# A split-product output projection, modulation sums moved into value products, and bias loads from another queue, in a four-layer transformer kernel

## The chip, the cores and the metric

One NeuronCore of one Trainium2 chip runs the whole program in one launch. The metric is the device time in microseconds (us). A profiled execution gives the trace; its times are read from one run.

## The reference

Four layers work on a sequence of 256 tokens of width 1024, in fp32. Each layer is a mixer and a mixture of experts, both added to the rows x. Layers 1 and 2 have 32 experts, layers 3 and 4 have 16. Layers 3 and 4 are modulated: `mod = silu(c) @ w_ada + b_ada` gives, for each of the two layers, six vectors of 1024 (shift, scale and gate of the mixer, shift, scale and gate of the experts), so `w_ada` is 1024 x 12288.

The change touches layer 3 above all, the dilated attention:

```
hm = rmsnorm(x, norm_mix) * (1 + sc_m) + sh_m
proj = (hm @ w_in).reshape(b, s, 3 groups, 3 of q/k/v, 16 heads, 64)
# for each group (window, dilation): logits = q.k + bias[bucket(distance)], masked, softmax
# the three groups of a head are merged by their softmax denominators
o = sum_g weight_g * out_g
x = x + g_m * (o @ w_out)
```

## The kernel before

**Stream.** All weights pass through one SBUF ring of 28672 fp32 columns per partition (14 slots of 1 MB). `Stream.add` lays the chunks out in the order of use, and gives each the number of chunks that must have been given back before it may be loaded (`need`). SyncE issues the loads (L96, `stream.issue`), waits on the counter `chunk_used`, and its last argument bounds for how many returned chunks it may wait at this point. An expert is three pieces of 1 MB. A chunk of `w_ada` is 3 MB, and there are 16 of them (`ada_at`); `weight_amid` places them between chunks of a weight. Layer 2's `w_out` has two 3 MB chunks, layer 3's `w_in` 18 chunks of 2 MB (nine for each half of the heads) and its `w_out` two of 2 MB.

**Modulation.** `ada_part` (L434 to L441) does the six sums of one `w_ada` chunk on VectorE, each a multiply with a row of silu(c) and a sum over 1024 columns (L438). The row is loaded by `load_silu_row` (L431). `modulation` turns the sums into `mod` and the gains. Before, chunks are summed in the output projections of layer 1 (3), 2 (2), 3 (3) and 4 (3), and five in input stages.

**Output projection.** `project_rows` (L452 on) does, for two 512-wide column blocks and two row blocks of 128 tokens, k fp32 matmuls of 128x128 by 128x512 each (L508; k is 12 in layer 2 and 8 in layer 3; the program runs each as two instructions). VectorE multiplies by the gate and adds to x (L1333, L1334), between its `ada_part` calls; ScalarE takes squares for the next norm (L543). With a gate, 8 small matmuls first spread it over rows (L500).

**Layer 3.** Two halves of eight heads, each of them `project_heads_split` and then `dilated_attention`. The first has nine jobs of 512 columns: q and k of three groups (six jobs, normed, scaled and transposed), then the value products of the three groups. Each weight row block is split in two fp32r halves: `high` is a copy by ScalarE (L859), `low` the difference by VectorE (L911). The same is done to the source (GpSimd makes its low part, L791). TensorE then does three products high*high, high*low and low*high (L826), six instructions for each of eight row blocks. There are three buffers for split weights, so `high` of block n waits for the products of block n-3.

`dilated_attention` (L1145 on) works on pairs of heads, i = 0 to 3. TensorE makes scores (L1187), transposes probabilities (L1220) and multiplies by the values (L1230). VectorE adds the bias and takes the extreme (L1260), scales (L1268) and copies the result out (L1287). ScalarE takes the exponentials (L1299) and copies the transposes out of PSUM (L1307, function `take`). Its order in one pass of the loop is two `take`s of pair i-1, `exp(i, 0)`, four `take`s of pair i-1, `exp(i, 1)`. The bias of a pair is six DMAs of 128 KB (L3091). The first two pairs are loaded during the value products; those of pairs 2 and 3 are issued by SyncE inside the attention, when the logits of pair i-2 are done:

```
@block.sync
def _(sp):
    for i in range(2, n):
        sp.wait_ge(*logits_ready[1].at(2 * (i - 1)))
        for y in range(2):
            bias_load(2 * i + y, bias[i][y], bias_loaded[i % 2].sem)
```

Every `nc.Block` ends with all engines meeting. After the projection comes `moe(2, ...)`, with 16 experts in eight pairs.

## Time and profile before

| what | value |
|---|---|
| median of 3 runs | 1508.71 us (1507.35 to 1511.42) |
| profiled execution, its own time | 1510.9 us |
| its span | 1509.2 us |
| mean granted TensorE clock | 0.984 |
| TensorE busy | 1410.7 us, 93% |
| VectorE, ScalarE, GpSimd busy | 736.5, 496.6, 103.0 us |
| DMA | 469.80 MB, mean 311 GB/s |

The stages by the trace: layer 2's output projection from 523 to 565 us, its experts until about 790; layer 3's first half with products from 801.5 to 907.6 and attention from 908.6 to 949.15; its second half with products from 951.0 to 1056.6 and attention from 1057.6 to 1098.67; its output projection from 1098.67 to 1130.16; its experts until 1241; then layer 4. A busy TensorE means that a matmul was in flight, not that the array was full; idle time of an engine that nobody waits for costs nothing.

### The profile page before, as it was taken

To read this page: it belongs to the slowest core of one execution; us is meant where nothing else is said; L and a number is where in the kernel's file an instruction comes from. 1 tells how busy PE (TensorE), PEld (TensorE's weight loads), DVE (VectorE), ACT (ScalarE), POOL (GpSimd) and SP (SyncE) were. 2 spreads that over 40 slices of the span, in tenths; PEclk is the share of its full clock that TensorE was granted. 3 is DMA by queue.
4 is the path that set the end of the run, shared out by engine and by line. 5 is a ranking of instruction groups with operands and counts; after the bars stand their busy time and mean duration, and the time that the engine had idled before them with its cause. 6 is when DMAs were issued, how large, how long until landed. Compare 5 with 4: busy or idle time off the path is not lost. (4 is left out here: it accounts for less than half of the span.)

```text
span 1509.2 us, 23584 instructions
## 1 busy us (share of the span) xinstructions
PE 1410.7 (93%) x9090; PEld 766.4 (51%) x9090; DVE 736.5 (49%) x1659; ACT 496.6 (33%) x996; POOL 103.0 (7%) x258
## 2 busy tenths in 40 slices
PE   8999999997899899999888997899799998989998
PEld 4486533332365645333226885788554337755432
DVE  1468332222255545222226765675576346669534
ACT  3222221111216403111116656665613126661211
POOL 0000021110000001111102000200001102000110
PEclk9999999999999999999999999999999999999999
DMA  8996989999974269999998463335369998437996
GB/s 365 366 348 265 405 360 411 420 420 421 427 301 167 97 290 370 398 422 420 421 423 347 168 251 112 112 140 192 116 243 419 420 425 324 162 119 296 422 420 247
DMA packets 63400, 469.80 MB, mean 311 GB/s; under 512 B 7809, under 2 KB 15921, under 8 KB 18738
## 3 DMA queue, kind: packets, MB, share of 16 engines
q1 hardware_dynamic: 63282, 468.22, 76.7%
q8 instruction: 75, 1.23, 0.3%
q14 instruction: 43, 0.35, 0.1%
HBM read 465.42 MB, written 2.76 MB: 310 GB/s over the span
## 5 line engine op out<-in xcount | busy, mean ns | idle before, releaser
L1663 PE MATMUL PS<-ring,catT 128*32 128x512 f32 x3072 | 347.9, 594 | 11.8 <-issue 10.9
L826 PE MATMUL PS<-w_split,h_split 128*128 128x512 f32 x1152 | 270.9, 394 | 6.0 <-DVE w_split L911 5.9
L826 PEld LDWEIGHTS PS<-w_split,h_split 128*128 128x128 f32 x1152 | 214.1, 188 | 56.5 <-DVE w_split L911 8.6
L1663 PEld LDWEIGHTS PS<-ring,catT 128*32 128x32 f32 x3072 | 96.0, 110 | 227.5 <-issue 227.2
L911 DVE TENSOR_TENSOR w_split<-ring,w_split 128x512 fp32r<-128x512 f32 x192 | 132.7, 706 | 67.3 <-ACT w_split L859 67.1
L1686 PE MATMUL PS<-ring,row_place 128*32 128x512 f32 x1232 | 141.8, 593 | 14.1 <-issue 14.1
L859 ACT CAST w_split<-ring 128x512 fp32r<-128x512 f32 x192 | 118.3, 621 | 104.5 <-PE PS L826 104.1
L1873 ACT ACTIVATE row_place<-PS 128x256 f32<-128x256 f32 x48 | 18.5, 385 | 359.7 <-PE PS L1663 359.7
L508 PE MATMUL PS<-ring,catT 128*128 128x512 f32 x224 | 96.7, 592 | 1.0 <-PEq L1022 1.0
L1686 PEld LDWEIGHTS PS<-ring,row_place 128*32 128x32 f32 x1232 | 40.9, 110 | 105.0 <-issue 104.4
L1556 POOL COPY catT<-xsT 128x256 f32 x176 | 63.3, 403 | 393.0 <-PE PS L1663 385.4
L2058 DVE TENSOR_TENSOR row_place<-PS,row_place 128x256 f32<-128x256 f32 x48 | 20.3, 422 | 130.8 <-ACT row_place L1873 130.8
L2062 DVE COPY row_place<-PS 128x256 f32<-128x256 f32 x48 | 20.4, 424 | 111.6 <-PE PS L1672 111.6
L508 PEld LDWEIGHTS PS<-ring,catT 128*128 128x128 f32 x224 | 42.3, 190 | 53.3 <-issue 53.3
L438 DVE CUSTOM_DVE_ANT_0 ring<-ring,row_place 128x1024 f32<-128x1024 f32 x48 | 55.6, 1223 | 5.9 <-DMA row_place<-silu_dram 5.5
L2083 DVE SCALAR_TENSOR_TENSOR gated_rows<-PS,slot_w,grow 128x512 f32<-128x512 f32 x32 | 24.0, 750 | 67.3 <-PE PS L1686 67.3
L2090 DVE SCALAR_TENSOR_TENSOR xn_split<-PS,slot_w,xn_split 128x512 fp32r<-128x512 f32 x36 | 27.0, 751 | 48.9 <-ACT xn_split L1860 48.9
L1537 POOL MEMSET xsT<- 128x512 f32 x4 | 2.1, 526 | 637.2 <-POOLq L476 507.7
L2605 PE MATMUL PS<-ring,catT 128*128 128x512 f32 x96 | 41.7, 594 | 1.3 <-DVE catT L2497 0.9
L438 DVE CUSTOM_DVE_ANT_0 ring<-ring,silu_row 128x1024 f32<-128x1024 f32 x36 | 41.7, 1222 | 1.3 <-PE PS L2404 1.3
L1860 ACT ACTIVATE xn_split<-PS,slot_w 128x512 fp32r<-128x512 f32 x36 | 24.8, 689 | 51.8 <-PE PS L1686 51.8
L791 POOL TENSOR_TENSOR h_split<-hT,h_split 128x256 fp32r<-128x256 f32 x24 | 24.3, 1023 | 232.9 <-ACT h_split L869 230.3
(445 smaller groups left out, 1829.4 us busy)
## 6 DMA issues: line engine op xcount, KB each, us to landing
ring<-in_moe SPq DMA_DIRECT2D x269, 1024.0 KB, 14.3
ring<-in_w_ada SPq DMA_DIRECT2D x16, 3072.0 KB, 13.0
ring<-in_a_w_in SPq DMA_DIRECT2D x23, 2048.0 KB, 10.4
ring<-in_b_w_in SPq DMA_DIRECT2D x8, 2048.0 KB, 22.5
first_down<-in_moe SPq DMA_DIRECT2D x8, 1024.0 KB, 8.4
ring<-in_a_w_out SPq DMA_DIRECT2D x2, 3072.0 KB, 15.2
ring<-in_b_w_out SPq DMA_DIRECT2D x2, 3072.0 KB, 16.5
ring<-in_w_mem_kv SPq DMA_DIRECT2D x2, 2048.0 KB, 11.6
```

The source lines that it names most:

```text
L438: last = nc.vector.tensor_tensor_reduce(w[:, m, :], w[:, m, :], row, 1.0, 0.0, ALU.mult, ALU.add, ada_out[:, 6 * c + m:6 * c + m + 1])
L508: last = nc.tensor.matmul(PS[:, i % 8, 0:n], srcT[:, j, t * P:(t + 1) * P], w[:, j, o:o + n], start=j == 0, stop=j == k - 1)
L791: nc.gpsimd.tensor_tensor(hs[:, 1, k, :], srcT[:, k, :], hs[:, 0, k, :].bitcast(F32), ALU.subtract).then_inc(h_low.sem, 1)
L826: last = nc.tensor.matmul(PS[:, 2 * (i % 2) + t, :], hs[:, hp, k, t * P:(t + 1) * P], wk[:, (KT * i + k) % splits, wp, :], start=k == 0 an ...
L859: nc.scalar.copy(wk[:, (KT * i + k) % splits, 0, :], w[:, k, :]).then_inc(w_high.sem, 1)
L911: nc.vector.tensor_tensor(wk[:, (KT * i + k) % splits, 1, :], w[:, k, :], wk[:, (KT * i + k) % splits, 0, :].bitcast(F32), ALU.subtract).t ...
L1556: nc.gpsimd.tensor_copy(xf[:, i % 2, :, q * HALF:(q + 1) * HALF], padded(q // 2)[:, :, bass.ds(at, HALF)]).then_inc(win_ready.sem, 1)
L1663: last = nc.tensor.matmul(PS[lanes, 4 + i % 2, :].rearrange("p (g f) -> p g f", g=2), xf[:, i % 2, k, lanes], gate_up_weights(2 * i + q % ...
L1686: last = nc.tensor.matmul(PS[lanes, 6 + c, :], hs[:, i % 2, f2, lanes], down_weights(2 * i + q % 2, f2)[:, c * BANK:(c + 1) * BANK], start ...
L1860: nc.scalar.activation(yk(i, 0, c), PS[:, 6 + c, :], ACT.Copy, scale=slot_w[:, i % 2, :]).then_inc(y_high.sem, 1)
L2090: nc.vector.scalar_tensor_tensor(yk(i, 1, c), PS[:, 6 + c, :], slot_w[:, i % 2, :], high, ALU.mult, ALU.subtract).then_inc(y_low.sem, 1)
L2605: last = nc.tensor.matmul(PS[:, bank, :], catT[:, k, t * P:(t + 1) * P], w[:, k, :], start=n == 0, stop=n == 11)
```

## The change

There are four edits.

1. Layer 3's output projection is done by a new function, `project_rows_split`, with the three fp32r products and four buffers for split weights. It has no modulation sums and doesn't load the silu row. The last three row blocks of the second column block are done for one row block of tokens and then for the other.
2. The three `w_ada` chunks that layer 3's output projection summed are gone from there. One is summed in each half, in the value products: one of its six sums behind the `low` of each of six weight blocks (jobs 7 and 8). ScalarE's queue issues the load of the silu row for it, behind the root of the last normed job, into the place of the squares.
3. The third goes to layer 2's output projection, which then sums three chunks in place of two: one ahead of the first column block, two ahead of the second.
4. The bias DMAs of pairs 2 and 3 are issued by ScalarE, behind `exp(i, 1)` of pairs 0 and 1; SyncE's loop is gone.

The order of chunks in the ring changes with 2 and 3.

```diff
-        c_bout = weight_amid("b_w_out", 12, [512] * 2, [1, 0], 1)
+        c_bout = weight_amid("b_w_out", 12, [512] * 2, [1, 1], 1)
-        c_ain2 = weight("a_w_in_2", 8, [512] * 18)
-        c_aout2 = weight_amid("a_w_out_2", 8, [512] * 2, [1, 0], 2)
+        c_ain2 = weight_amid("a_w_in_2", 8, [512] * 18, [0] * 8 + [1] + [0] * 8 + [1])
+        c_aout2 = weight("a_w_out_2", 8, [512] * 2)
...
+        def ada_sum(c, m, row):
+            w = stream.view(ada_at[c], 6)
+            return nc.vector.tensor_tensor_reduce(w[:, m, :], w[:, m, :], row, 1.0, 0.0, ALU.mult, ALU.add, ada_out[:, 6 * c + m:6 * c + m + 1])
...
+        def project_rows_split(srcT, k, first, gate, router, after, gain=None, shift=None, splits=4):
...
+                HELD = 3
+                @block.sync
+                def _(sp):
+                    wr, br = router_weights(router)
+                    nc.sync.dma_start(wr, A[f"wr{router}"]).then_inc(r_loaded.sem, 16)
+                    nc.sync.dma_start(br, A[f"br{router}"].partition_broadcast(P)).then_inc(r_loaded.sem, 16)
+                    stream.issue(nc, sp, first)
+                    load_early_down(router, (0, 1))
...
+                    stream.issue(nc, sp, first + 1)
+                @block.gpsimd
+                def _(pool):
+                    for j in range(k):
+                        pool.wait_ge(*(h_odd if j % 2 else h_even).at(j // 2 + 1))
+                        nc.gpsimd.tensor_tensor(hs[:, 1, j, :], srcT[:, j, :], hs[:, 0, j, :].bitcast(F32), ALU.subtract).then_inc(h_low.sem, 1)
+                @block.tensor
+                def _(pe):
+                    def product(c, j, t, h, w):
+                        return nc.tensor.matmul(PS[:, 2 * c + t, :], hs[:, h, j, t * P:(t + 1) * P], wk[:, (k * c + j) % splits, w, :],
+                                                start=j == 0 and h == 0 and w == 0, stop=j == k - 1 and h == 1)
...
+                    for c in range(2):
+                        held = k - HELD if c else k
+                        for j in range(held):
+                            if c == 0:
+                                pe.wait_ge(*(h_odd if j % 2 else h_even).at(j // 2 + 1))
+                            pe.wait_ge(*w_high.at(k * c + j + 1))
+                            for t in range(TT):
+                                product(c, j, t, 0, 0)
+                            pe.wait_ge(*w_low.at(k * c + j + 1))
+                            for t in range(TT):
+                                product(c, j, t, 0, 1)
+                            if c == 0:
+                                pe.wait_ge(*h_low.at(j + 1))
+                            for t in range(TT):
+                                last = product(c, j, t, 1, 0)
...
+                            last.then_inc(w_used.sem, 1)
+                        for t in range(TT if held < k else 0):
+                            for j in range(held, k):
...
+                                for h, w in ((0, 0), (0, 1), (1, 0)):
+                                    last = product(c, j, t, h, w)
+                            last.then_inc(rows_ready.sem, 1)
...
+                @block.scalar
+                def _(act):
...
+                    nc.scalar.activation(stat[:, 2, 30:31], ones_f[:, 0:1], ACT.Sqrt)
+                    for j in range(0, k, 2):
+                        nc.scalar.copy(hs[:, 0, j, :], srcT[:, j, :]).then_inc(h_even.sem, 1)
+                        high(0, j)
+                        high(0, j + 1)
+                    for j in range(k):
+                        high(1, j)
+                    for i in range(3):
+                        square(i)
...
+                    for j in range(0, k, 2):
+                        nc.vector.tensor_copy(hs[:, 0, j + 1, :], srcT[:, j + 1, :]).then_inc(h_odd.sem, 1)
+                        low(0, j)
+                        low(0, j + 1)
+                        if j == 4:
...
+                                nc.vector.tensor_copy(gain, PS[:, 6:8, :].rearrange("p b n -> p (b n)")).then_inc(gate_made.sem, 1)
...
+                            after()
+                    for j in range(k):
+                        low(1, j)
+                        if j == splits - 1:
+                            add(0)
+                        if j == splits:
+                            add(1)
+                    add(2)
+                    add(3)
...
 # project_heads_split, ScalarE and VectorE
+                            if sums_behind and i == turns[-1]:
+                                nc.scalar.dma_start(silu_row, A["silu_dram"].to_broadcast([P, D])).then_inc(silu_loaded.sem, 16)
...
+                            if (i, k) in sums_behind:
+                                m = sums_behind.index((i, k))
+                                if m == 0:
+                                    dve.wait_ge(*silu_loaded.at(16))
+                                    dve.wait_ge(*stream.landed(ada_at[ada_chunk]))
+                                last = ada_sum(ada_chunk, m, silu_row)
+                                if m == 5:
+                                    dlink(last)
+                                    nc.vector.sem_inc(chunk_used, 1)
...
 # dilated_attention
-                @block.sync
-                def _(sp):
-                    for i in range(2, n):
-                        sp.wait_ge(*logits_ready[1].at(2 * (i - 1)))
-                        for y in range(2):
-                            bias_load(2 * i + y, bias[i][y], bias_loaded[i % 2].sem)
...
                         if i < n:
                             exp(i, 1)
+                        if i + 2 < n:
+                            act.wait_ge(*logits_ready[1].at(2 * (i + 1)))
+                            for y in range(2):
+                                bias_load(nc.scalar, 2 * (i + 2) + y, bias[i + 2][y], bias_loaded[i % 2].sem)
...
-            project_rows(catT, 12, c_bout, [512] * 2, add_rows(None), ada=[1, 0], ada_last=1, ...)
+            project_rows(catT, 12, c_bout, [512] * 2, add_rows(None), ada=[1, 1], ada_last=1, ...)
...
+                        project_heads_split(hT, c_ain2 + half * 10, jobs, ..., ada_chunk=11 + half, sums_behind=((7, 3), (7, 5), (7, 7), (8, 1), (8, 3), (8, 5)), ...)
...
-            project_rows(catT, 8, c_aout2, [512] * 2, add_rows(grow[:]), ada=[1, 0], ada_last=2, after=..., router=2, gate=mod[:, 0, 16:24], shift=mod[:, 0, 24:32])
+            project_rows_split(catT, 8, c_aout2, mod[:, 0, 16:24], 2, lambda: modulation(1, (0, 24), (0,)), grow[:], mod[:, 0, 24:32])
```

## Rows read from the trace of the kernel before

**Rows 1.** Page, part 1: busy time of each engine, share, instructions.

```profile
PE 1410.7 (93%) x9090; PEld 766.4 (51%) x9090; DVE 736.5 (49%) x1659; ACT 496.6 (33%) x996; POOL 103.0 (7%) x258
```

**Rows 2.** Busy by window: stretch, length, PE, PEld, DVE, ACT, POOL, clock, DMA.

```profile
1098.67:1130.16 31.49, 31.18 (x96) 15.81 (x96) 27.79 (x47) 3.67 (x8) 0.00 (x0) 1.00 0.76 286
908.60:949.15 40.55, 31.81 (x312) 23.66 (x312) 21.82 (x60) 24.40 (x58) 0.00 (x0) 0.92 0.21 76
1130.16:1241.00 110.84, 109.84 (x963) 43.44 (x965) 52.57 (x143) 24.23 (x44) 12.94 (x38) 1.00 1.00 416
```

**Rows 3.** Timeline of layer 3's output projection: start, length, engine, line.

```profile
1098.68 1.28 ACT L528 ACT_TABLE_LOAD   x1 [2.99 <-PEq L1153]
1100.58 27.63 PE L508 MATMUL PS<-ring,catT 128*128 128x512 f32 x64
1128.36 0.70 DVE L1333 TENSOR_TENSOR PS<-PS,grow 128x512 f32<-128x512 f32 x1 [0.25 <-PE PS L508]
```

**Rows 4.** Groups by line, value products of the second half, 1034 to 1058.

```profile
L826 PE MATMUL PS<-w_split,h_split 128*128 128x512 f32 x96 | 22.0, 390 | 0.0
L911 DVE TENSOR_TENSOR w_split<-ring,w_split 128x512 fp32r<-128x512 f32 x14 | 9.7, 693 | 9.6 <-ACT w_split L859 9.6
L859 ACT CAST w_split<-ring 128x512 fp32r<-128x512 f32 x14 | 8.7, 624 | 8.9 <-PE PS L826 8.9
```

**Rows 5.** Timeline, start of the second half's products.

```profile
949.15 0.41 ACT L869 CAST h_split<-hT 128x256 fp32r<-128x256 f32 x1 [3.00 <-PEq L1153]
951.05 11.17 PE L826 MATMUL PS<-w_split,h_split 128*128 128x512 f32 x48 [2.67 <-DVE w_split L911]
```

**Rows 6.** Timeline: two neighbouring modulation sums.

```profile
1103.69 1.22 DVE L438 CUSTOM_DVE_ANT_0 ring<-ring,row_place 128x1024 f32<-128x1024 f32 x1
1104.83 1.22 DVE L438 CUSTOM_DVE_ANT_0 ring<-ring,row_place 128x1024 f32<-128x1024 f32 x1
```

**Rows 7.** Bias DMA issues (L3091) on SyncE: ns min/median/max.

```profile
L3091 SPq DMA_DIRECT2D z_rows<-bias_dram x24: 567/570/1462, 885.8 to 1066.8; - x24
```

**Rows 8.** Timeline of the first half's attention, behind `exp(0, 1)`.

```profile
914.40 4.56 SPq L3091 DMA_DIRECT2D z_rows<-bias_dram  x6
915.38 0.84 ACT L1307 COPY catT<-PS 128x384 f32<-128x384 f32 x2
916.91 1.54 PE L1220 MATMUL PS<-ident,logits 128*128 128x128 f32 x6 [1.78 <-DVE logits L1268]
917.85 0.48 ACT L1307 COPY probsT<-PS 128x384 f32<-128x384 f32 x1 [0.43 <-PE PS L1220]
```

**Rows 9.** The same, behind `exp(1, 1)`; the last is from the second half.

```profile
924.11 1.78 SPq L3091 DMA_DIRECT2D grow<-bias_dram  x3
925.00 0.19 ACT L1299 ACTIVATION_READ_ACCUMULATOR logits<-logits,rowmax 128x1 f32 x1
925.70 0.86 ACT L1307 COPY catT<-PS 128x384 f32<-128x384 f32 x2 [0.51 <-PE PS L1220]
927.71 0.88 PE L1220 MATMUL PS<-ident,logits 128*128 128x128 f32 x6 [1.08 <-DVE logits L1268]
928.29 0.86 ACT L1307 COPY probsT<-PS 128x384 f32<-128x384 f32 x2 [0.53 <-PE PS L1220]
1075.24 0.86 ACT L1307 COPY catT<-PS 128x384 f32<-128x384 f32 x2 [1.00 <-PE PS L1220]
```

**Rows 10.** Timeline of layer 2's output projection: VectorE's last adds.

```profile
554.22 0.69 DVE L1334 TENSOR_TENSOR x<-x,PS 128x512 f32<-128x512 f32 x1 [2.10 <-PE PS L508]
564.63 0.69 DVE L1334 TENSOR_TENSOR x<-x,PS 128x512 f32<-128x512 f32 x1 [9.72 <-PE PS L508]
```

**Rows 11.** Windows of layer 2's projection and of its experts' end.

```profile
550.00:560.00 10.00, 10.00 (x24) 4.37 (x23) 2.74 (x8) 0.73 (x2) 0.00 (x0) 1.00 0.45 186
560.00:570.00 10.00, 9.28 (x49) 6.07 (x47) 4.74 (x9) 3.59 (x6) 0.53 (x1) 1.00 0.35 121
740.00:760.00 20.00, 16.39 (x142) 5.49 (x142) 4.08 (x9) 2.30 (x4) 1.43 (x4) 1.00 1.01 422
```

More of the change, by code:

```diff
@@ L741, in project_heads, with project_heads_split @@
                 s.passed(k)
-        def project_heads_split(srcT, first, jobs, splits=3, rows=None, norm=None, side=None, load_last=None):
+        def project_heads_split(srcT, first, jobs, splits=3, rows=None, norm=None, side=None, load_last=None, ada_chunk=None, sums_behind=()):
             turns = [i for i, job in enumerate(jobs) if job["hd"]]
@@ L767, in turned_x @@
                     return PS[:, 4 + 2 * (k % 2) + k // 4, at:at + T]
+                silu_row = catT[:, 8:12, :].rearrange("p k n -> p (k n)")
                 def chunk(i):
-                    return first + i + (1 if side is not None and i >= 3 else 0)
+                    return first + i + (1 if side is not None and i >= 3 else 0) + (1 if sums_behind and i >= len(jobs) - 1 else 0)
                 def col16(q):
@@ L958, in project_heads_split @@
                 s.passed(k)
+            silu_loaded.passed(16 if sums_behind else 0)
             for s in (w_high, w_low, w_used):
@@ L3060, in build @@
                 attention([mla_head(h) for h in range(8)], True, row_scale=qs[:, 2])
-            project_rows(catT, 12, c_bout, [512] * 2, add_rows(None), ada=[1, 0], ada_last=1, after=lambda: modulation(0, (0, 48), (0, 1)), router=1)
+            project_rows(catT, 12, c_bout, [512] * 2, add_rows(None), ada=[1, 1], ada_last=1, after=lambda: modulation(0, (0, 48), (0, 1)), router=1)
         if stop >= 4:
@@ L3085, in build, with bias_load @@
                         bias = [(first_bias[:, 0], first_bias[:, 1]), (other_bias, catT[:, 5:8, :])]
-                        def bias_load(h, dst, loaded):
+                        def bias_load(eng, h, dst, loaded):
                             bd = A["bias_dram"]
@@ L3095, in load_two_biases @@
                                 for y in range(2):
-                                    bias_load(2 * i + y, bias[i][y], sig(f"bias_loaded{i}").sem)
-                        project_heads_split(hT, c_ain2 + half * 9, jobs, rows=z_rows, load_last=load_two_biases,
+                                    bias_load(nc.sync, 2 * i + y, bias[i][y], sig(f"bias_loaded{i}").sem)
+                        project_heads_split(hT, c_ain2 + half * 10, jobs, rows=z_rows, load_last=load_two_biases, ada_chunk=11 + half, sums_behind=((7, 3), (7, 5), (7, 7), (8, 1), (8, 3), (8, 5)),
                                             norm=(mod_gain[:, 0, 0, :], mod[:, 0, 0:8]) if half == 0 else None)
@@ L3106, in build @@
                         dilated_attention([head(h) for h in range(8)], bias, bias_load)
-            project_rows(catT, 8, c_aout2, [512] * 2, add_rows(grow[:]), ada=[1, 0], ada_last=2, after=lambda: modulation(1, (0, 24), (0,)), router=2, gate=mod[:, 0, 16:24], shift=mod[:, 0, 24:32])
+            project_rows_split(catT, 8, c_aout2, mod[:, 0, 16:24], 2, lambda: modulation(1, (0, 24), (0,)), grow[:], mod[:, 0, 24:32])
         if stop >= 7:
```

62 lines of the change are left out of this document (61 added, 1 removed).

## The prediction

> **What bounds the kernel now.** I read the page's first part, then the busy time by windows, then the timeline of the stages that the diff touches. TensorE is busy 1410.7 of 1509.2 us [rows 1], but that is no single limit. In layer 3's output projection it never stops (31.18 of 31.49 us) [rows 2], and the timeline shows one unbroken run of 27.63 us of fp32 matmuls, with VectorE's last gate product starting 0.25 us behind it [rows 3]: TensorE sets that stage, and VectorE's 27.79 busy us there, mostly modulation sums, lie under it. Layer 3's experts are set by TensorE too (109.84 of 110.84), although DMA is full (share 1.00) [rows 2]. The experts of layer 2 are different: from 740 to 760 TensorE has 16.39 of 20 us at 422 GB/s [rows 11]; there DMA decides. The attention is set by a ring of short steps through four engines: TensorE has 31.81 of 40.55 us at clock 0.92 [rows 2], and each step waits for another engine [rows 8, 9].
>
> **Output projection: -4.4 us.** It removes the 27.63 us run [rows 3]. In its place are 2 column blocks x 8 row blocks x 6 = 96 products. The value products ran 96 of the same in 22.0 us with no idle [rows 4], so that is the new run, 5.6 us less. It begins later. The old run began 1.91 us behind the stage's start at 1098.67. The new one needs, on ScalarE in turn, the table load (1.28, and 0.20 for the operation that calls it), a source copy 0.41 [rows 3, 5] and a weight copy 0.62, then VectorE's difference of 0.69 [rows 4]: first products at 2.6, and the low part at 3.3, when the first two products (0.46) are done and wait 0.3. That is as if the run began 2.9 behind the stage's start, 1.0 later; with 0.2 for the first block, where the second half's 48 products took 11.17 in place of 11.0 [rows 5], the net is -5.6 + 1.0 + 0.2 = -4.4. The feeders keep up: of 1.38 us that TensorE takes for a block, ScalarE needs 0.62 and half a source copy (0.2), VectorE 0.69 and half of one, and four buffers leave about three blocks of lead; the gate copy and the first adds (about 1.4 us each) fit into it. GpSimd's low parts are needed in the first block alone. The tail (router matmuls, last gate product and add) stays. Bounds: -5.6 with no start loss, -2.5 if VectorE's inserted adds are felt.
>
> **Sums in the value products: +0.5 us.** Two sums start 1.14 us apart [rows 6], so with the reading out of the sum I take 1.15 to 1.23. VectorE is busy 0.69 of each 1.38 us block [rows 4]. A sum behind every second block asks 2 x 0.69 + 1.2 = 2.6 of 2.75 us. The worst place is job 7, block 5, where a sum is followed by the last copy out of a transposed bank (0.7): the next low part is 0.69 + 1.2 + 0.7 - 1.38 = 1.2 us late. TensorE bears about 1.4: with three buffers a high part starts when the block three before is done, 0.62 + 0.69 + hops give 1.35, and TensorE comes to it after two blocks, 2.75. So nearly nothing shows; I take 0.25 per half. If nothing were hidden it would be 12 x 1.2 = 14 us, and I keep 4 of that as the upper end. The silu row's load is one issue on ScalarE, which idles 8.9 of 24 us there [rows 4].
>
> **The third chunk in layer 2: 0.** VectorE gets six more sums, 6.9 us, ahead of its add at 554.22, which would push that at most to 561.1, still ahead of the last one at 564.63, which waits 9.72 us for TensorE [rows 10]. The 3 MB go into the ring ahead of experts' pieces, before a stage that DMA decides; 3 MB at 420 GB/s are 7.5 us. But of the 20 us from 550 to 570, DMA is idle 0.55 and 0.65 of the time [rows 11], 12 us, since the ring is full. Going through `need` for both orders, 14 pieces of the experts are in the ring when the projection ends, in both kernels, and the next piece waits for the same event. The delayed 4 MB (the chunk and its place) fit into the idle 12 us. Its price if the cover failed is the 7.5 us.
>
> **Ring in layer 3: 0.** Three chunks fewer ahead of layer 3's experts let 10 pieces be loaded during the half's products, against none before the projection now. It buys nothing: TensorE waits for no DMA there [rows 2].
>
> **Bias loads on ScalarE: +6.5 us.** No row shows a DMA issued by ScalarE. The nearest rows are SyncE's for the same transfers: 0.57 us each at the median, 1.46 at most [rows 7]. Six make 3.4 us. Behind them on ScalarE stands `take(i, 0)`, for which TensorE's third transpose of the pair waits, since the PSUM bank must be free, and through it the ring of steps. The wait that the change adds is met already when `exp(i, 1)` starts (ScalarE waited for the same count), so I take it that the issue starts there, beside the exponential. For i = 0: from 914.40 to 917.8; `take` ran at 915.38, and the later `take` had 0.43 us of wait to give [rows 8], so 2.0 by ScalarE's order, 1.7 with what TensorE at its lower clock would need anyway. For i = 1: from 924.11 to 927.5; `take` ran at 925.70 with 0.53 to give later [rows 9], 1.3; in the second half `take` was 0.5 later in relation (idle 1.00 against 0.51 [rows 9]), 0.8. Sum over both halves: 1.7 + 1.7 + 1.3 + 0.8 = 5.5. Before, six transposes took 1.54 us at 916.91, after a pause of 1.78 us [rows 8], and 0.88 at 927.71 [rows 9]: TensorE was at the lower of its two levels in the first place (clock 0.92 over the stage [rows 2]). Longer pauses may lengthen that; I add 1.0. Lower bound: 1.1 us if an issue takes 0.33, as the plain loads of SyncE do, and 0 below that; nothing can be gained, since no VectorE instruction waited for a bias. Upper bound: 13 us, with SyncE's 4.56 us for six [rows 8], begun only when the exponential has ended. I take the same cost as on SyncE because the transfers are the same.
>
> The Trainium skill has two rules that pull apart here. "DMA: Bandwidth & Descriptors", section "Issuing engines are not separate DMA queues", says that spreading issues over engines only saves the sequencer's issue time, usually small beside the transfer; by it the edit costs little, and the sum would be about -3.9. "Perfetto Trace Analysis", section "Per-engine timelines", says that an issuing sequencer is held until the descriptors are generated; by it ScalarE is held as long as SyncE, which is the sum taken here. The rows of SyncE (0.57 us each) agree with the second so far as they go.
>
> **Sum.** -4.4 + 0.5 + 0 + 0 + 6.5 = +2.6 us on the profiled execution, whose own time is 1510.9. That run lies 2.2 us above the median of 1508.71; the difference is taken over unchanged: 1511.3.
>
> **Rivals.**
> - *Issue is cheap on ScalarE (0.25).* An issue of up to about 0.34 us would end before the `take` behind it plus its slack (2.1 us at i = 1), and the attention keeps its time. Then only -4.4 + 0.5 = -3.9 remain: 1504.8. For it: the descriptor work may differ. Against it: the same transfers took 0.57.
> - *The issues are felt in full (0.25), the slower side.* Place: the four issue groups in the attention. If the six issues start only when the exponential is done (925.19, 1.0 us later than the wait), each adds 1.0: +4, together +6.6, 1515.3; with more time at the lower clock 1518. It decides from the point where the last issue ends 4.2 us after its wait is met: then the four delays exceed the 3.9 us gained by 4.5.
> - *VectorE doesn't keep up in the value products (0.08).* Each sum that is felt costs up to 1.2; with 4 us, 1515. For it: 2.6 of 2.75 us asked. Against it: six sums only, and 9.6 us of idle [rows 4].
> - That the new projection doesn't gain: only if the split parts come late; the rows of the same feeders in the same order show no idle of TensorE [rows 4].
>
> **How the numbers follow.** A difference of 0.3%, 4.5 us, is about what can be told from no change. The forecast case (0.42) has its own range from 1507 to 1514. Of it 0.02 is faster, 0.33 within the bound, 0.07 slower. The cheap issue gives 0.12 faster, 0.13 same, since -3.9 lies close to the bound. Full cost: 0.23 slower, 0.02 same. VectorE: half and half. Sum: faster 0.14, same 0.52, slower 0.34. For 8 in 10 I reach from 1503.5 to 1517.
>
> **What would show it.** In the trace after: products of 22 to 22.6 us in the projection, begun 2.6 us behind its start, and the stage about 27 in place of 31.5 us; ScalarE's DMA issues of about 0.57 us each, and an idle or a lag of `take` behind `exp(i, 1)`; attentions of 43 to 44.5 us in place of 40.55 and 41.1; product stages of the halves unchanged within 0.5 us; layer 2's experts and layer 3's experts of unchanged length. The prediction is wrong if issues on ScalarE are much shorter or don't hold back the next `take`, if TensorE's low clock lasts far longer in the attention, or if layer 2's experts end later.

## The result, and the profile after

The changed kernel takes 1521.7 us (median of 11 runs, 1512.64 to 1526.39), the kernel before in the same comparison 1510.74 (11 runs, 1502.79 to 1514.76): ratio 1.007, 95% interval 1.0053 to 1.0088. The prediction said 1511.3 us, in a range from 1503.5 to 1517.0; the change is slower by 11 us, not by 2.6. The profiled execution of the changed kernel took 1517.79 us, 3.9 under its median; its span is 1515.8, 6.6 us above the span before, so it shows somewhat over half of the loss by medians.

First the page's line of busy times and the new queue, for the changed kernel; they answer to [rows 1]. The columns of the last line are packets, MB and share of 16 engines.

```profile
PE 1412.5 (93%) x9117; PEld 777.7 (51%) x9122; DVE 750.0 (49%) x1679; ACT 506.3 (33%) x1016; POOL 111.8 (7%) x266
q10 hardware_dynamic: 3552, 4.20, 0.9%
```

TensorE is 1.8 us busier in all, although the run of products in its projection is 5 us shorter (22.68 against 27.63, below), so its busy time has grown elsewhere. Where the added time sits is seen when the changed kernel's layer 3 is cut at the first matmul of each stage: attention of the first half, projection and value products of the second half, its attention, output projection, router, experts. The last three columns are granted clock, DMA share and GB/s.

```profile
908.40:956.40 48.00, 33.12 (x313) 24.75 (x313) 23.02 (x63) 26.14 (x62) 1.45 (x2) 0.86 0.28 104
956.40:1062.90 106.50, 104.71 (x482) 85.47 (x482) 77.14 (x117) 63.10 (x109) 7.23 (x7) 1.00 0.55 205
1062.90:1107.43 44.53, 33.31 (x312) 24.58 (x312) 21.83 (x60) 24.22 (x57) 0.00 (x0) 0.89 0.36 136
1107.43:1134.60 27.17, 26.35 (x129) 21.65 (x130) 21.16 (x32) 14.31 (x29) 8.75 (x9) 1.00 0.44 159
1134.60:1152.80 18.20, 17.95 (x115) 15.11 (x117) 14.88 (x51) 9.03 (x17) 1.73 (x6) 0.81 0.48 174
1152.80:1255.60 102.80, 97.33 (x865) 31.94 (x866) 42.80 (x104) 20.86 (x41) 11.14 (x32) 0.99 0.98 402
```

The kernel before, cut in the same way, at the two attentions, the router stage and the experts (its projection stands in [rows 2]):

```profile
908.60:951.00 42.40, 31.81 (x312) 23.66 (x312) 22.94 (x63) 26.25 (x62) 1.37 (x2) 0.92 0.21 72
1057.70:1098.67 40.97, 32.28 (x312) 24.08 (x312) 21.82 (x60) 24.32 (x57) 0.00 (x0) 0.92 0.25 92
1130.16:1146.30 16.14, 15.15 (x113) 12.65 (x114) 14.72 (x50) 9.06 (x16) 1.81 (x6) 1.00 0.95 383
1146.30:1248.70 102.40, 97.29 (x864) 31.89 (x865) 42.85 (x104) 20.93 (x41) 11.13 (x32) 0.99 1.01 422
```

By these rows the two attentions are 5.6 and 3.6 us longer, the projection is 4.4 shorter, the router stage behind it 2.1 longer, and the experts 0.4. The second half's products are 106.5 (before 106.6), and layer 3 starts within 0.1 us of where it did. Together that is +7.3; from first to last matmul the program is 6.9 longer, the rest being tenths either way.

The same rows tell waiting from slow work. In the two attentions together TensorE is busy 66.43 us where it was busy 64.09, and idle 26.10 (length less busy time) where it was idle 19.28. So of the 9.2 us 6.8 are waits, and 2.3 are matmuls that took longer, which with the same instructions is the lower clock.

The first group of issues, on ScalarE of the changed kernel (start, duration; ACTq is its instruction queue; in brackets the idle time before and what ended it):

```profile
914.15 1.18 ACTq L3251 DMA_DIRECT2D z_rows<-bias_dram  x1
914.21 0.92 ACT L1455 ACTIVATE logits<-logits,rowmax 128x768 f32<-128x768 f32 x1
915.37 4.29 ACTq L3251 DMA_DIRECT2D z_rows<-bias_dram  x5
919.70 0.86 ACT L1463 COPY catT<-PS 128x384 f32<-128x384 f32 x2 [4.49 <-issue]
```

The issues occupy 914.15 to 919.66, 5.5 us. The first goes beside the exponential, the other five behind it, and the copy of the transposes comes at 919.70 where [rows 8] has it at 915.38. In the second half the same six take 3.7 us (1068.66 to 1072.38) and the copy comes at 1072.43. The first groups of both halves together (shortest, median and longest in ns):

```profile
L3251 ACTq DMA_DIRECT2D z_rows<-bias_dram x12: 581/590/1477, 914.2 to 1071.8; - x12
```

TensorE's side: the step before that copy and the one behind it, the step where the second group is felt, and the first group's place in the second half:

```profile
914.17 0.82 PE L1343 MATMUL PS<-dkT,dqT 64*128 64x256 f32 x4 [0.87 <-DVE rowmax L1416]
920.33 1.51 PE L1376 MATMUL PS<-ident,logits 128*128 128x128 f32 x6 [5.33 <-ACT catT L1463]
931.54 1.38 PE L1376 MATMUL PS<-ident,logits 128*128 128x128 f32 x6 [1.80 <-ACT catT L1463]
1073.05 1.51 PE L1376 MATMUL PS<-ident,logits 128*128 128x128 f32 x6 [3.67 <-ACT catT L1463]
```

The kernel before at the last of these places:

```profile
1065.94 1.54 PE L1220 MATMUL PS<-ident,logits 128*128 128x128 f32 x6 [1.79 <-DVE logits L1268]
```

TensorE waits 5.33 us in the first half, 1.78 in [rows 8], and 3.67 against 1.79 in the second. The second groups add less: 1.80 and 1.73 against 1.08 in both halves before ([rows 9] for the first). Those four, 3.55 + 1.88 + 0.72 + 0.65, are the 6.8 us of waits. At 931.54 six transposes take 1.38, where [rows 9] has 0.88: here the clock has fallen a second time. Cut by clock, the changed kernel and then the kernel before:

```profile
915.00:926.00 11.00, 5.67 (x34) 4.06 (x36) 2.96 (x9) 3.98 (x12) 0.00 (x0) 0.55 0.35 118
926.00:931.00 5.00, 3.73 (x49) 2.87 (x44) 3.88 (x12) 2.03 (x5) 0.00 (x0) 1.00 0.22 56
931.00:936.00 5.00, 4.46 (x22) 3.00 (x22) 0.92 (x3) 3.68 (x10) 0.00 (x0) 0.66 0.29 101
```

```profile
915.00:921.00 6.00, 4.21 (x18) 2.80 (x16) 2.56 (x8) 3.86 (x11) 0.00 (x0) 0.52 0.43 129
921.00:931.00 10.00, 8.92 (x89) 6.38 (x90) 5.77 (x16) 6.21 (x15) 0.00 (x0) 0.95 0.26 81
```

Before there is one stretch of some 6 us at the lower level (1.2 GHz), after there are two, of 10 and 3.5 us. Most of what the first has grown by costs nothing: up to 920.33 TensorE only waits in it, and the work behind that wait runs at the lower level for about 4.5 us, against about 5 in the kernel before (916.91 to 922). What the clock adds in this half is the second stretch. Last, the projection and what follows it on TensorE in the changed kernel:

```profile
1109.89 22.68 PE L624 MATMUL PS<-w_split,h_split 128*128 128x512 f32 x96 [0.40 <-ACT w_split L674]
1136.34 4.51 PE L1737 MATMUL PS<-catT,hT 128*128 128x20 f32 x32
1140.68 3.76 PE L1742 MATMUL PS<-ident,mod 128*128 128x128 f32 x16
```

The run of 22.68 us answers to the 27.63 of [rows 3]. The 16 spreading matmuls of the router stage take 3.76 us; in the kernel before the same take 2.03, all at full clock.

### The profile page after: what moved, and what is told of

The parts are those of the page before. It is cut to its first block and busy times, and to the rows that moved or that the text cites. A ratio compares the mean times of both kernels' runs of the same rounds, so it can differ in the third digit from the quotient of the medians.

```text
span 1515.8 us, 23699 instructions
## 1 busy us (share of the span) xinstructions
PE 1412.5 (93%) x9117; PEld 777.7 (51%) x9122; DVE 750.0 (49%) x1679; ACT 506.3 (33%) x1016; POOL 111.8 (7%) x266
## 5 line engine op out<-in xcount | busy, mean ns | idle before, releaser
L1823 PE MATMUL PS<-ring,catT 128*32 128x512 f32 x3072 | 347.9, 594 | 11.4 <-issue 11.3
L2218 DVE TENSOR_TENSOR row_place<-PS,row_place 128x256 f32<-128x256 f32 x48 | 20.3, 422 | 129.9 <-ACT row_place L2033 129.9
L513 PE MATMUL PS<-ring,catT 128*128 128x512 f32 x160 | 69.1, 593 | 1.1 <-PEq L1185 1.1
L513 PEld LDWEIGHTS PS<-ring,catT 128*128 128x128 f32 x160 | 30.2, 190 | 38.5 <-issue 38.5
L438 DVE CUSTOM_DVE_ANT_0 ring<-ring,row_place 128x1024 f32<-128x1024 f32 x36 | 41.7, 1221 | 4.4 <-DMA row_place<-silu_dram 4.0
L1376 PE MATMUL PS<-ident,logits 128*128 128x128 f32 x144 | 25.3, 322 | 19.8 <-ACT catT L1463 12.5
L2765 PE MATMUL PS<-ring,catT 128*128 128x512 f32 x96 | 41.7, 594 | 1.1 <-DVE catT L2657 0.9
## 6 DMA issues: line engine op xcount, KB each, us to landing
ring<-in_b_w_in SPq DMA_DIRECT2D x8, 2048.0 KB, 19.3
```

The costliest lines, as they stand in the source:

```text
L438: last = nc.vector.tensor_tensor_reduce(w[:, m, :], w[:, m, :], row, 1.0, 0.0, ALU.mult, ALU.add, ada_out[:, 6 * c + m:6 * c + m + 1])
L513: last = nc.tensor.matmul(PS[:, i % 8, 0:n], srcT[:, j, t * P:(t + 1) * P], w[:, j, o:o + n], start=j == 0, stop=j == k - 1)
L1376: last = nc.tensor.transpose(PS[:, 6 + c % 2, s * P:(s + 1) * P], logits(i, t, y)[:, s, kt * P:(kt + 1) * P], ident[:])
L1823: last = nc.tensor.matmul(PS[lanes, 4 + i % 2, :].rearrange("p (g f) -> p g f", g=2), xf[:, i % 2, k, lanes], gate_up_weights(2 * i + q % ...
L2765: last = nc.tensor.matmul(PS[:, bank, :], catT[:, k, t * P:(t + 1) * P], w[:, k, :], start=n == 0, stop=n == 11)
```

## The experiments

All times are medians, with the ratio to the kernel before on the same chip and its 95% interval. "Attentions" are the two stages of layer 3 in the run's own profile, from first matmul to first matmul. (The expectations of e1 and e2 count the first one to its own last matmul, 40.6 before and 46.1 after.) g3 is the changed kernel itself, so its 46.5 against 48.0 tells by how much a stage differs from profile to profile. Other parts differ more: with nothing changed ahead of it, the first attention starts at 903.2 in e1, 907.6 in g3 and 913.3 in g1, and layer 4's attention, projection and router stages, which no run changes, take 75.9 to 82.7 us together. So the total of a single profile says little.

| run | time, us | ratio | interval | attentions, us |
|---|---|---|---|---|
| kernel before | 1509.3 to 1510.7 | 1 | | 42.4, 41.1 |
| changed kernel | 1521.7 | 1.007 | 1.0053 to 1.0088 | 48.0, 44.6 |
| e1: loads on SyncE | 1510.65 | 1.0009 | 0.9984 to 1.0034 | 42.2, 42.3 |
| e2: only the loads moved | 1520.55 | 1.0087 | 1.0065 to 1.011 | 45.1, 44.2 |
| e3: e1, fp32 projection | 1511.55 | 1.0019 | 1.0001 to 1.0037 | 42.7, 40.9 |
| e4: half the issues moved | 1512.54 | 1.0029 | 1.0013 to 1.0046 | 43.7, 41.6 |
| f1: changed, fillers in the holds | 1514.29 | 1.0026 | 1.0002 to 1.005 | 45.1, 42.7 |
| f2: e1, fillers at the router | 1509.53 | 1.0001 | 0.9978 to 1.0024 | 42.6, 40.4 |
| f3: issues three and three | 1511.98 | 1.0007 | 0.9982 to 1.0032 | 42.9, 39.8 |
| f4: e1, fillers in both places | 1513.94 | 1.0018 | 0.9991 to 1.0044 | 41.4, 43.8 |
| g1: e1, copies as long as the issues | 1516.38 | 1.0036 | 1.0018 to 1.0054 | 47.9, 44.6 |
| g2: issues spread thinly | 1510.3 | 1.0005 | 0.9983 to 1.0026 | 42.4, 41.1 |
| g3: changed kernel again | 1521.1 | 1.0066 | 1.004 to 1.0093 | 46.5, 44.2 |

**Which edit costs the time (e1 to e4).** e1 takes the issues off ScalarE and leaves the rest of the change:

```diff
+@block.sync
+def _(sp):
+    for i in range(2, n):
+        sp.wait_ge(*logits_ready[1].at(2 * (i - 1)))
+        for y in range(2):
+            bias_load(nc.sync, 2 * i + y, bias[i][y], bias_loaded[i % 2].sem)
...
-    if i + 2 < n:
-        act.wait_ge(*logits_ready[1].at(2 * (i + 1)))
-        for y in range(2):
-            bias_load(nc.scalar, 2 * (i + 2) + y, bias[i + 2][y], bias_loaded[i % 2].sem)
```

> The kernel after with its bias loads of pairs 2 and 3 back on SyncE, all else kept. Theory A (ScalarE's sequencer is held by six issues of about 0.6 us, behind which the next take stands): both attentions return to the lengths of before, 40.6 and 41.1 us in place of 46.1 and 44.6, so the time falls by about 9 us against the kernel after, to 1508 or 2 us under the kernel before. Theory B (SyncE's queue is backed up by 10 MB of expert pieces, and bias loads behind them come late in the second half): VectorE waits for a bias at pair 2 of the second half, and that attention stays 3 us or more above 41.1. Theory C (the attention is longer since TensorE's clock is lower for another reason): nothing changes, 1.007 of before.

e2 is the converse: the kernel before with only those lines moved to ScalarE.

> The kernel before with edit 4 alone. Theory A: attentions of 44.5 to 46.5 us each, 9 us over the kernel before, ratio 1.006. Theory C or any in which the moved sums and the ring matter: no more than 3 us over it. Should the ratio be 1.009 or more, the lengths of the attention are not all that it costs.

e3 is e1 with the fp32 projection put back.

```diff
-project_rows_split(catT, 8, c_aout2, mod[:, 0, 16:24], 2, ...)
+project_rows(catT, 8, c_aout2, [512] * 2, add_rows(grow[:]), ..., router=2, ...)
```

> The kernel after with bias loads on SyncE and with the old fp32 projection of layer 3, so the moved modulation sums are all that is left of the change. If these are free, the same as the kernel before within 1.5 us, and its projection stage is again 31.5 us. If TensorE's clock falls in the router stage behind the projection because the projection is a run of fp32r products, then here that stage (from the end of the projection to the first product of the experts) is 16.1 us as before, and 18.2 in e1_bias_sync; if it falls by chance or for the DMA's sake, the two are alike.

e4 leaves the loads of y = 0 on ScalarE and issues those of y = 1 from SyncE.

```diff
-for y in range(2):
-    bias_load(nc.scalar, 2 * (i + 2) + y, ...)
+bias_load(nc.scalar, 2 * (i + 2), bias[i + 2][0], ...)      # y = 1: the same on SyncE
```

> The kernel after with three of the six bias loads of a pair issued by ScalarE and three by SyncE. Theory A, with about 2.1 us of cover behind exp(1, 1) and 1.4 behind exp(0, 1): three issues take 1.8 us, so at i = 1 nothing is felt and at i = 0 about 0.5 us; both attentions are within 1.5 us of before. If the cost is in proportion to the number of issues, without cover, each attention is 2 to 2.8 us over before.

Measured: e1 is back at the time before, and e2 alone has the whole loss. So the moved bias loads cost 0.6% (after against e1) to 0.9% (e2), 9 to 13 us by the ratios and 10 to 11 by the medians, and edits 1 to 3 together are worth nothing that can be measured. In e1's second half (42.3, before 41.1) VectorE waits for a bias, as its Theory B had it, though less than the 3 us named there; more on this under f4. Half the issues (e4) cost a sixth to a third of the loss (1.9 of 11 us by medians, 0.2 of 0.6% by ratios) and 0.8 us in the attentions over e1, where all six cost 8.1 in the changed kernel; the intervals of the times would still allow a cost in proportion. The attentions of e2, and of g3 below it, split the cost again:

```profile
905.20:950.30 45.10, 31.07 (x312) 23.24 (x313) 22.96 (x63) 25.90 (x62) 1.40 (x2) 0.92 0.20 69
1058.30:1102.50 44.20, 32.93 (x312) 24.67 (x313) 21.81 (x60) 24.19 (x58) 0.00 (x0) 0.88 0.24 86
```

```profile
907.60:954.00 46.40, 31.05 (x312) 23.23 (x313) 22.95 (x63) 25.88 (x62) 1.40 (x2) 0.92 0.28 108
1062.00:1106.20 44.20, 32.95 (x312) 24.70 (x312) 21.83 (x60) 24.20 (x57) 0.00 (x0) 0.88 0.36 136
```

TensorE is busy 64.0 us in both, no more than before (64.09), and idle 25.3 and 26.6 (before 19.3). So with the whole group of issues in one place the added 6.0 to 7.3 us of waiting is there in each of the three profiles, the added work at the low clock only in one of them. e2's attentions are 5.9 us longer and its time 10.4: the lengths of these stages are not all of the timed cost.

e3 shows what the new projection gives back. Its projection and router stages:

```profile
1093.50:1125.00 31.50, 31.20 (x97) 15.82 (x98) 7.15 (x12) 3.65 (x9) 0.09 (x1) 1.00 0.44 153
1125.00:1141.10 16.10, 15.09 (x116) 12.62 (x120) 14.73 (x51) 9.04 (x17) 1.71 (x6) 1.00 0.54 196
```

and e1's router stage behind the fp32r projection:

```profile
1122.90:1141.10 18.20, 17.95 (x112) 15.39 (x114) 14.73 (x50) 9.03 (x17) 1.75 (x6) 0.81 0.48 174
```

The router stage is 16.1 us in all three profiles with the fp32 projection (before, e2, e3), at clock 1.00. With the fp32r one it is 18.2 or 18.3 in seven (after, e1, e4, f1, g1, g2, g3) and 16.6 in f3, where the clock fell late (0.90 over the stage); f2 and f4, which add matmuls there, have 18.8 and 17.2.

**Hold or low clock (f1), and number or length (f3, g2).** f1 puts filler matmuls where TensorE waits for the issues:

```diff
 if i < n:
     scores1(i, 0)
+if i in (1, 2):
+    for _ in range(30 if i == 1 else 18):
+        nc.tensor.matmul(PS[:, 3, 256:512], zero[:], ones_b[:, 0:1].to_broadcast([P, 256]), ...)
```

> The changed kernel with matmuls that compute nothing (bf16, 256 columns, into columns of a PSUM bank that nobody reads) put where TensorE waits for ScalarE's six bias issues: 30 behind the first pair of heads, 18 behind the second, in both halves. At full clock they take 3.2 and 1.9 us, and lie inside the waits of 5.3 and some 2.6 us. Theory A (the issues cost ScalarE's hold and nothing else): the two attention stages stay at about 48.0 and 44.6 us, the time at the changed kernel's 1521. Theory B (a good part of the cost is the low clock that the idle TensorE gets behind the wait, seen in transposes at 1.5 us for six instead of 0.88): six transposes behind the first wait come at about 0.88, the stages at about 44 to 45.5 and 42 to 43 us, the time some 4 to 6 us under the changed kernel's, 1515 to 1517.

In the first half of f1's trace (TensorE) the fillers run at full clock, and the transposes behind the wait keep it:

```profile
909.41 3.50 PE L1382 MATMUL PS<-ones_b,zero 128*128 128x256 bf16 x30
914.72 0.85 PE L1376 MATMUL PS<-ident,logits 128*128 128x128 f32 x6 [1.81 <-ACT catT L1470]
```

In the second half the clock fell just before the fillers began (0.60 from 1062 to 1063, the fillers from 1063.08), and the 30 took 4.71 us. The stages are 45.1 and 42.7, the time 1514.29, as Theory B had it. Of the changed kernel's loss 0.4% (7 us) goes with fillers alone, though ScalarE is held about as long as before (the copy still waits 4.28 us for the issues). But in the first half the fillers also took away the low stretch that the kernel before has, so this is what a full clock gives back there; it doesn't show that the low clock caused so much of the loss, and by the busy times above it caused 2.3 us at most.

f3 keeps all six issues on ScalarE and splits them: three where they were, three behind the next pair's first exponential.

```diff
 if i < n:
     exp(i, 0)
+if 0 < i < n - 1:
+    bias_load(nc.scalar, 2 * (i + 1) + 1, bias[i + 1][1], ...)
```

> The changed kernel with its six bias issues a pair still all on ScalarE, but three behind the exp of rows 128 to 255 and three behind the next pair's exp of rows 0 to 127. The number of issues is the same, only the longest hold is halved. Theory A (each issue costs what it holds, 0.58 us, wherever it stands): no change, attention stages 48.0 and 44.6, time 1521. Theory B (what counts is the length of one hold: a short one hides in the time in which ScalarE waits for transposes anyway and does not let the clock fall, as with three issues, where the stages were 43.7 and 41.6): stages of about 44 to 46 and 42 to 43 us, time 1513 to 1517.

Measured 1511.98, ratio 1.0007: the loss is gone with the same issues on the same queue, so neither their number nor the queue nor the transfers make it. ScalarE of f3, at the first group:

```profile
915.24 1.85 ACTq L3252 DMA_DIRECT2D z_rows<-bias_dram  x2
917.14 0.48 ACT L1463 COPY catT<-PS 128x384 f32<-128x384 f32 x1 [2.05 <-issue]
917.29 0.63 ACTq L3252 DMA_DIRECT2D z_rows<-bias_dram  x1
```

The hold is 2.05 in place of 4.49 us, and the later issues go beside the copies and exponentials. The attentions are 42.9 and 39.8, and TensorE is idle 20.3 us in them, 26.1 in the changed kernel and 19.3 before:

```profile
908.24:951.10 42.86, 31.35 (x312) 23.27 (x313) 22.96 (x63) 26.12 (x62) 1.40 (x2) 0.92 0.31 116
1059.30:1099.10 39.80, 31.04 (x312) 23.23 (x313) 21.82 (x60) 24.35 (x58) 0.00 (x0) 0.96 0.39 149
```

g2 spreads them further, two, one, one, one and one:

```diff
+if 0 < i < n - 1: issue(i + 1, 0, 2)        # ahead of exp(i, 0)
 if i < n:
     exp(i, 0)
+if 0 < i < n - 1: issue(i + 1, 1, 0)
 for j in range(2, 6):
     take(i - 1, j)
+    if i < n - 1 and j in (3, 5): issue(i + 1, 1, j // 2)
```

> The changed kernel with its six issues a pair still all on ScalarE, spread thinner: two behind the exp of rows 128 to 255, and one each ahead of and behind the next pair's exp of rows 0 to 127, behind its third and fifth copy of transposes. If only the length of one hold counts, this is at least as good as three and three: stages of about 42 to 43 and 40 to 42 us, 1509 to 1513 (before: 1509 to 1510). If each issue costs what it holds: stages of 44 to 46 us in both halves, 1515 to 1520.

It has 1510.3 us and stages of 42.4 and 41.1, the same as f3 within the intervals and the same as the kernel before. Both runs change the length of a hold and its place together; which of the two frees it is not separated, and what the rows show is that the waits are gone.

**Is it the DMA issue at all (g1, g3).** g1 has the loads on SyncE and holds ScalarE with useless copies instead:

```diff
 if i < n:
     exp(i, 1)
+if i + 2 < n:
+    for k in range(11 if i == 0 else 6):
+        alink(nc.scalar.copy(held[:], ones_f[:, 0:1].to_broadcast([P, T])))
```

> The changed kernel with the bias loads on SyncE, and in their place on ScalarE eleven copies (128x256) into a buffer that nobody reads behind the first pair of heads and six behind the second, in both halves: by the copies of that size in the profile some 0.4 us each, 4.5 and 2.5 us, as long as the holds by the issues. Theory A (the cost is the hold of ScalarE, whatever holds it, with the low clock behind it): the attention stages come to about 48 and 45 to 48 us, the time to about 1519 to 1523. Theory B (it is the DMA issuing itself, its transfers by another queue or their collision with the ring's): stages and time stay with the kernel that has the loads on SyncE, 42.2 and 42.3 us plus at most a microsecond or two, 1511 to 1513.

> The changed kernel once more, beside the two others: the anchor for them. By both theories as it was: stages of 48.0 and 44.6 us or within 1.5 us of that, about 1520, a ratio of 1.006 to 1.009.

ScalarE and TensorE of g1, to be read beside the changed kernel's rows above:

```profile
920.04 4.74 ACT L1486 COPY held<-ones_f 128x256 f32<-128x256 f32 x11
924.81 0.86 ACT L1471 COPY catT<-PS 128x384 f32<-128x384 f32 x2
```

```profile
925.43 1.51 PE L1384 MATMUL PS<-ident,logits 128*128 128x128 f32 x6 [5.40 <-ACT catT L1471]
```

```profile
913.29:961.20 47.91, 33.08 (x313) 24.59 (x313) 22.98 (x63) 32.74 (x79) 1.42 (x2) 0.86 0.27 104
1067.70:1112.30 44.60, 31.08 (x312) 23.30 (x313) 21.83 (x60) 30.72 (x75) 0.00 (x0) 0.92 0.35 133
```

In the first half the wait (5.40 against 5.33), the slow transposes and the stage (47.9 against 48.0) are the changed kernel's: there a hold by copies costs what a hold by DMA issues costs. In the second half the stages agree (44.6) but not their parts: the eleven copies make TensorE wait 5.64 us where the issues made it wait 3.67, and its busy time is 31.08 us in place of 33.31. By the timing g1 is slower than the kernel before (1.0036) and above e1 (1.0009), by some 4 us, but 4.7 us under the changed kernel measured beside it (1521.1); the intervals, 1.0018 to 1.0054 and 1.004 to 1.0093, overlap. The expected 1519 to 1523 is missed, on the cheap side, by a kernel that is held longer in all. So that a hold of ScalarE, by whatever work, lengthens the attention is shown; that it is the whole of the timed loss is not.

**The router stage (f2, f4).** Fillers of 512 columns, two ahead of the router's products and three between their halves:

```diff
+if m == 2:
+    keep_busy(7, 2)
 pe.wait_ge(r_loaded.sem, 32 * (m + 1))
 for t in range(TT):
+    if m == 2 and t == 1:
+        keep_busy(7, 3)
```

> The changed kernel with the bias loads back on SyncE (1510.65 us), plus two and three matmuls that compute nothing (bf16, 512 columns) ahead of and between the two token halves of the router's products behind the third layer's output projection; they cost 1.1 us of TensorE at full clock. Theory A (the router stage there is 18.2 us instead of 16.1 because the clock falls behind a long stretch of 20-column products): the clock stays at 1.00 through the stage, the 16 spreading matmuls take 2.0 instead of 3.8 us, the stage comes to about 16.5 to 17.3 us, the experts' stage to 102.4. Net gain 1 to 2 us, which the timing can hardly tell. Theory B (the stage is longer because of what the transfers or VectorE do there): the stage stays at 18.2 or grows by the 1.1 us to 19.3.

> The changed kernel with the bias loads back on SyncE, the five 512-column fillers of the router stage, and 14 fillers of 256 columns (1.5 us at full clock) in both attention stages at the one place where the clock fell there, ahead of the first pair's transposes of rows 128 to 255. If the low clock behind the first pair is what makes the attention's first 10 us slow, the stage goes from 42.2 to about 39 to 41 us and the time to about 1506 to 1508, under both kernels; if the fillers only lengthen what waits, the stage stays at 42 to 43.5 and the time at 1510 to 1512.

f2 misses: the clock falls all the same and the stage is longer, as Theory B there had it, though not by its reason. The window of f2's stage:

```profile
1119.80:1138.50 18.70, 18.43 (x116) 15.68 (x118) 14.81 (x50) 8.98 (x16) 1.74 (x6) 0.82 0.47 170
```

Its spreading matmuls take 3.76 us, as in the changed kernel.

f4 adds fillers in the attention of e1 as well. The first attention gains 0.8 us over e1 (41.4), the second loses 1.5 (43.8), and the time, 1513.94, lies above both of its expectations. The 14 fillers of the first half took 3.00 us in place of 1.5: the clock fell as they began (1.00 from 916 to 917, 0.51 from 917 to 919). The loss in the second is another thing, seen on VectorE of f4, where the third pair's bias is added:

```profile
1075.52 0.56 DVE L1430 CUSTOM_DVE_ANT_1 logits<-PS,z_rows 128x384 f32<-128x384 f32 x1 [3.25 <-DMA z_rows<-bias_dram]
```

VectorE waits 3.25 us for a bias issued by SyncE. The same wait is 1.11 us in e1, 1.62 in e3 and 1.20 in f2; it is absent in the kernel before, in the changed one, f3, g1 and g2. The issues come as early as before (5.8 us behind the stage's start in all), and in e1, e3, f2 and f4 VectorE can go on 10.8 to 11.4 us behind the first of them. The kernel before comes for this bias only 11.5 us behind its first issue, g1 14.0 us, so they would see no wait even if their loads took as long: the wait is as long as VectorE comes early, and f4, quickened by its fillers, comes first (8.1 us). Whether the loads also land later than they did before is not shown; f3, whose ScalarE issues them, finds them there 10.2 us behind the first. The stage's DMA share is 0.36 to 0.39 in these runs, 0.25 before, so more of the ring's transfers run beside them; no run takes the ring's loads away. No version beats the kernel before by more than its interval; the best are f2 and g2, level with it.

## Why the prediction was wrong

By the medians the miss has two parts of like size. Edits 1 to 3 were to give -3.9 us, and e1, which has them alone, is level with the kernel before (+0.5). The moved bias loads were to cost 6.5, and cost 10.4 (e2) to 11 (the changed kernel against e1).

**Output projection: right at its place, wrong behind it.** Predicted -4.4, measured -4.4 (27.1 in place of 31.5), with the run of products at 22.68 (22 to 22.6 were expected) begun 2.4 behind the stage's start (2.6 expected). What the prediction left at "the tail stays" is the stage after: 2.1 us in the router stage, because TensorE's clock falls in the router's small matmuls (0.81 over the stage, 1.00 before), and 0.4 in the experts. Net -1.9 in the profile. That the fp32r projection brings the fall is shown by e3 against e1, 16.1 against 18.2, and by the other profiles; why the clock falls behind the one run and not behind the other is open, and fillers of 1.1 us do not stop it. The 0.4 us of the experts are not the clock: TensorE is busy 97.33 us there (before 97.29), and the time is lost at their end, where VectorE starts on the norm's sums 0.4 us later; the reason is open. In the timing e1 (1510.65) and e3 (1511.55, with the fp32 projection) can't be told apart.

**Sums in the value products, third chunk, ring: right.** Predicted +0.5, 0 and 0. The second half's products are unchanged (106.5 us) and layer 3 starts at 801.7 (before 801.6). The rival in which VectorE doesn't keep up is out. One side effect was missed that the loads on ScalarE then hid: with SyncE's loads VectorE waits 1.1 us or more for a bias in the second half (e1, e3).

**Bias loads on ScalarE: the step that failed.** The mechanism was named rightly: ScalarE is held, the `take` behind it is late, TensorE waits, and longer waits lengthen the time at the low clock. The size was wrong: 5.5 for the hold and 1.0 for the clock, and the stages grew by 9.2 us in the profile.
- The hold. The four delays were put at 1.7, 1.7, 1.3 and 0.8; TensorE's waits grew by 3.55 and 1.88 (first groups) and 0.72 and 0.65 (second groups), 6.8 in all. So one delay was mis-sized, the first half's first group. Its six issues were to end 3.4 us from their wait, at 917.8, by the median of [rows 7]; they took 5.5. The first took 1.18 beside the exponential and the other five 4.29. The other groups kept the expected pace: 3.7 us in the second half, and about 0.6 each for the second group (927.23 to 930.87). The prediction had taken 4.56 for six on SyncE at this very place [rows 8] for an upper end; that row, from the same moment of the program and not the median over all, was nearer.
- The clock. The cost of 1.0 us was a guess. In this profile it is 2.3 (busy 66.43 against 64.09), in e2 and g3 it is nothing (64.0), so the guess lies inside what the profiles show.

With the hold untouched and the clock kept up (f1) the stages lose 4.8 of the 9.2 us and the time 7 of 11; that is a gain which the kernel before could have had in part, and no measure of the clock's share in the loss.

"Perfetto Trace Analysis", section "Per-engine timelines", of the Trainium skill holds an issuing sequencer until the descriptors are generated; the rows agree so far as they go, since ScalarE's next instruction stood behind issues of 0.58 us each and up to 1.48. By "DMA: Bandwidth & Descriptors" of the Trainium skill, section "Issuing engines are not separate DMA queues", the issue time is usually small beside the transfer. The conclusion that the prediction tried from it, the cheap-issue rival, failed: by it the whole change would have taken 1504.8, and it took 1521.7. Once the issues are spread (f3, g2) they cost nothing that can be measured.

**The rival on the slower side** (felt in full, 1515.3 to 1518) was nearest, and right in its place. Its reason was that the issues start only when the exponential is done. The first started beside it (914.15, the exponential 914.21), the next at 915.37 behind it. Its deciding point, the last issue ending more than 4.2 us behind its wait, was passed by one group of four (5.5; the others 3.7 and 3.6). Its price was still short of the median by 4 us.

**What stays open.** The profiled execution carries 6.9 us of the 11, and e2's attentions 5.9 of its 10.4. Where the rest of the timed loss lies is not shown. g3, whose profiled run (1520.96) is at its median, has a span 9.6 us above the kernel before's; 7.2 of them are the attentions, and layer 4's attention, projection and router stages are 4.5 longer there (80.4 against 75.9). But those stages take 80.9 in e3 and 82.7 in e1 too, which have no loss, so this may be chance: layer 4's router stage alone, untouched by the change, varies from profile to profile between 16.1 and 21.0 us. The granted clock over all runs is 0.978 for the changed kernel, 0.983 for e1 and 0.985 for the kernel before, so the other runs too have more time at the low level.

## What to carry to other kernels

A DMA issued by a compute engine is work of that engine: cost it by the nearest row from the same moment, put it where the engine waits anyway, and spread a group of issues so that no single hold outlasts the slack of what stands behind it; here three and three were free and six in a row cost 0.6 to 0.9%. To tell waiting from a low clock, compare the idle and the busy time of the stage over several profiles: a longer stretch at the low level costs nothing while the engine only waits in it. When a stage that ran at full clock is shortened or its instructions change, look at the granted clock of the stage behind it before counting the gain.

## What the runs showed of the hardware that was not expected

- Matmuls that compute nothing won back half of what a stall had cost: 30 of 256 columns (3.50 us) in a wait of 5.3 us kept the clock at 1.00, and six transposes at 0.85 instead of 1.51 us (f1). Where the clock fell as they began or just before, they took up to double time (14 in 3.00 us in f4, 30 in 4.71 in the second half of f1).
- ScalarE issues a DMA beside its own running instruction: the single issues between copies and exponentials (f3, g2) mostly left no gap, while of six in one place only the first or the first two went beside the exponential.
- Behind the fp32r projection the clock of one and the same stage fell in every profile, once late; behind the fp32 one in none of three. TensorE was busy nearly throughout in both (17.95 of 18.20 and 15.09 of 16.10 us).
